# Row requests of a product-key expert layer in another order: the first table one group ahead, the second table with sixteen slots at the end

## What is computed

```python
def one_chunk(xc):                      # 128 tokens
    q = (xc @ w_query).reshape(C, 8, 2, 128)
    s = einsum('chpd,hpnd->chpn', q, subkeys)
    s1, i1 = top_k(s[:, :, 0], 16); s2, i2 = top_k(s[:, :, 1], 16)
    top_s, top_c = top_k(all sums of s1 and s2, 16)
    idx = i1[top_c // 16] * 128 + i2[top_c % 16]
    act = gelu(einsum('chkd,cd->chk', u_tbl[idx], xc))
    coef = softmax(top_s) * act
    return einsum('chk,chkd->cd', coef, v_tbl[idx])
```

## Time and profile before

| | |
|---|---|
| time, median of 3 runs | 1553.29 us (1553.16 to 1553.7) |
| time of the profiled execution | 1554.89 us |
| its span on the core | 1553.1 us |

### The profile page before, as it was taken

One profiled execution on the slowest core, in us unless ns is written; L12 is line 12 of the kernel. 1 busy time (PEld: TensorE's weight loads), 2 busy tenths in 40 slices (PEclk: granted clock), 3 DMA queues, 4 the chain that ended last, 5 costly groups with the idle time before them and its releaser, 6 DMA issues.

```text
span 1553.1 us, 13591 instructions
## 1 busy us (share of the span) xinstructions
PE 1035.4 (67%) x4216; PEld 471.9 (30%) x4216; DVE 1036.3 (67%) x2716; ACT 397.5 (26%) x920; POOL 974.2 (63%) x1041
## 2 busy tenths in 40 slices
PE   9998877655846767736675688787757774444444
PEld 8984422221213332212221334333212221111111
DVE  3367667775777484837676757377778677767673
ACT  1122132222222323222321232333222332112122
POOL 0067757776766655756666665467757767777772
PEclk9999978887967987878887788988979787766667
DMA  9699999999999999999999999999999999999996
GB/s 330 200 343 391 406 406 409 407 406 403 409 409 406 398 405 402 382 407 405 407 406 404 385 401 402 396 373 409 406 406 409 409 410 409 410 409 409 409 409 243
DMA packets 194636, 607.57 MB, mean 391 GB/s; under 512 B 17596, under 2 KB 44292, under 8 KB 194564
## 3 DMA queue, kind: packets, MB, share of 16 engines
q0 software_dynamic: 147456, 536.94, 87.3%
q1 hardware_dynamic: 46976, 69.73, 12.7%
q10 hardware_dynamic: 132, 0.04, 0.0%
HBM read 605.59 MB, written 1.05 MB: 391 GB/s over the span
## 4 chain that ended last, share of the span: by engine, by line
DMA 35%; PE 21%; POOL 17%; DVE 14%; issue 8%; ACT 5%; DVEq 0%; POOLq 0%; ACTq 0%
DMA rows<-in_peer_u,expert 18%; DMA rows<-in_peer_v,expert_v 16%; POOL rows L682 10%; PE sums L967 8%; DVE rows L1820 7%; POOL rows L675 7%; PE banks L783 4%; PE banks L799 4%; DVE coef L1837 2%; ACT soft_diag L1346 1%; PE banks L792 1%; PE sums L792 1%; DMA wring<-in_attn_w_q 1%; PE banks L775 0%; ACT L1331 0%
## 5 line engine op out<-in xcount | busy, mean ns | idle before, releaser
L967 PE MATMUL sums<-rows,soft_diag 128*64 128x512 f32 x2048 | 583.6, 724 | 446.9 <-ACT soft_diag L1346 446.6
L1820 DVE SCALAR_TENSOR_TENSOR rows<-rows,xn_near 128x1024 f32<-128x1024 f32 x512 | 612.6, 1219 | 253.3 <-DMA rows<-in_peer_u,expert 241.3
L682 POOL DMA_INDIRECT rows<-in_peer_v,expert_v x512 | 489.6, 956 | 295.4 <-PE sums L967 159.0
L675 POOL DMA_INDIRECT rows<-in_peer_u,expert x512 | 481.9, 941 | 258.9 <-issue 126.5
L967 PEld LDWEIGHTS sums<-rows,soft_diag 128*64 128x64 f32 x2048 | 162.7, 164 | 841.9 <-ACT soft_diag L1346 541.1
L1346 ACT ACTIVATE soft_diag<-stacked,coef 128x64 f32<-128x64 f32 x512 | 160.7, 343 | 369.8 <-DMA rows<-in_peer_v,expert_v 296.7
L1338 ACT ACTIVATE gelu<-dots 128x8 f32<-128x8 f32 x64 | 13.3, 208 | 446.1 <-DVE rows L1820 444.2
L799 PE MATMUL banks<-wring,xT 128*128 128x512 f32 x160 | 77.3, 636 | 3.4 <-DMA wring<-in_attn_w_q 3.4
L1837 DVE SCALAR_TENSOR_TENSOR coef<-gelu,gate_inv,gate 64x4 f32<-64x4 f32 x256 | 56.8, 222 | 23.4 <-ACT gelu L1338 19.5
L1885 DVE SCALAR_TENSOR_TENSOR soft_diag<-banks,soft_diag 128x512 f32<-128x512 f32 (+1 forms) x8 | 7.7, 958 | 92.7 <-ACT soft_diag L1367 92.7
L783 PE MATMUL banks<-xT,rows 128*128 128x128 f32 x448 | 51.1, 276 | 1.3 <-issue 0.6
(11 more groups left out here) (230 smaller groups left out, 958.6 us busy)
## 6 DMA issues: line engine op xcount, KB each, us to landing
wring<-in_w_kv SPq DMA_DIRECT2D x14, 1024.0 KB, 16.9
rows<-in_peer_u,expert POOLq DMA_INDIRECT x512, 15.0
rows<-in_peer_v,expert_v POOLq DMA_INDIRECT x512, 14.4
wkept<-in_peer_w_query SPq DMA_DIRECT2D x8, 1024.0 KB, 13.7
rows<-in_conv_w_in SPq DMA_DIRECT2D x7, 1024.0 KB, 11.9
wring<-in_peer_w_query SPq DMA_DIRECT2D x7, 1024.0 KB, 13.1
wring<-in_attn_w_q SPq DMA_DIRECT2D x7, 1024.0 KB, 16.5
wkept<-in_conv_w_out SPq DMA_DIRECT2D x4, 1024.0 KB, 12.5
```

The costliest lines, as they stand in the source:

```text
L675: nc.gpsimd.indirect_dma_start(u_row[j], None, u_table, bass.IndirectOffsetOnAxis(ap=expert[n % 2][:, k:k + 1], axis=0)).then_inc(u_landed ...
L682: nc.gpsimd.indirect_dma_start(v_row[j], None, v_table, bass.IndirectOffsetOnAxis(ap=expert_v[n % 2][:, k:k + 1], axis=0)).then_inc(v_land ...
L967: last = nc.tensor.matmul(sums[side * HP:(side + 1) * HP, half, :], diag[:, g * GROUP + j, :], v_row[j][:, half * 512:(half + 1) * 512], s ...
L1820: nc.vector.scalar_tensor_tensor(out=u_row[j], in0=u_row[j], scalar=1.0, in1=xn_near[:, :, :].rearrange("p a d -> p (a d)"), op0=ALU.mult, ...
```

## The change

POOL's queue is put in another order. Before: u0 v0 u1 v1 u2 v2 u3 v3 ... (each a group of 8 rows). Now: u0 v0 u1, then row by row v(1, 0) u(2, 0) v(1, 1) u(2, 1) ..., then u3 v2 u4 v3 ... u62 v61, then row by row u(63, 0) v(62, 0) u(63, 1) ..., then v63. The wait for the experts of group 2 stands ahead of the first v(1, j). The number of gathers is the same, 512 of each table.

PE's `combine_in_slot(K)` takes group K for K = 0 and 1, nothing at K = 2, and group K-1 after that. ACT's `weigh(K)` now makes four diagonals of group K-1, the gelu of group K, and the other four (all eight first, at the last group). DVE makes the coefficients after the next experts have been found or after the slot's mixer work, where before it made them right after the dots. `expert_v`, the second table's indices, has three buffers where it had two.

From group 49 on, every second group of the second table goes into eight further slots, `spare_rows`, which lie in two thirds of the weight ring, `keyT` and `value`; a v pair then waits for `v_used` of the group before the last.

```diff
+        spare_rows = [a.rearrange("p a t -> p (a t)")[:, D * half:D * (half + 1)]
+                      for a in (wring[:, 0], wring[:, 1], keyT[:, :, :], value[:, :, :]) for half in range(2)]
...
+        FIRST_LATE = GROUPS
+        LAST_GROUP = GROUPS * STEPS - 1
...
-            first_group()
-            for K in range(1, GROUPS * STEPS):
-                gather_group(K // GROUPS, K % GROUPS)
+            def experts_of(K):
+
+                if K == 1:
+                    pool.wait_ge(expert_ready, 2)
+                elif K % GROUPS == 0:
+                    pool.wait_ge(expert_ready, K // GROUPS + (2 if K else 1))
...
+            def second_row(K, j):
+
+                n, g = divmod(K, GROUPS)
+                if j % 2 == 0:
+                    if K == TWO_SETS + 1:
+                        wait_filled(pool, "queries", 1, 1)
+                    elif K:
+                        pool.wait_ge(v_used, TWOS * (K - 1 if K <= TWO_SETS else K - 2) + j // 2 + 1)
...
+            first_rows(0)
+            second_rows(0)
+            first_rows(1)
+            experts_of(FIRST_LATE)
+            for j in range(GROUP):
+                second_row(FIRST_LATE - 1, j)
+                first_row(FIRST_LATE, j)
+            for K in range(FIRST_LATE + 1, LAST_GROUP):
+                first_rows(K)
+                second_rows(K - 1)
+            second_experts_of(LAST_GROUP - 1)
+            for j in range(GROUP):
+                first_row(LAST_GROUP, j)
+                second_row(LAST_GROUP - 1, j)
+            second_rows(LAST_GROUP)
...
+            def combine_in_slot(K):
+
+                if K != FIRST_LATE:
+                    n, g = divmod(K if K < FIRST_LATE else K - 1, GROUPS)
+                    combine(n, n % 2, g)
...
+                K = GROUPS * n + g
+                early = GROUP if K == LAST_GROUP else GROUP // 2
+                if K > FIRST_LATE:
+                    diagonals(K - 1, range(early))
                 act.wait_ge(dot_done, TOPK * n + ks.stop)
                 nc.scalar.activation(gelu[b][:, ks], dots[b][:, ks], ACT.Gelu).then_inc(gelu_done, 1)
+                if K > FIRST_LATE and early < GROUP:
+                    diagonals(K - 1, range(early, GROUP))
+                if K < FIRST_LATE:
+                    diagonals(K, range(GROUP))
```

More of the change, by code:

```diff
@@ L439, in trunk @@
         expert = [sb(f"expert{b}", [P, TOPK], U32) for b in range(2)]
-        expert_v = [sb(f"expert_v{b}", [P, TOPK], U32) for b in range(2)]
+        expert_v = [sb(f"expert_v{b}", [P, TOPK], U32) for b in range(3)]
         top = [sb(f"top{b}", [P, TOPK]) for b in range(2)]
@@ L527, in trunk @@
         u_landed = [sem(f"u_landed{j}") for j in range(U_SLOTS)]
-        v_landed = [sem(f"v_landed{j}") for j in range(V_SLOTS)]
+        v_landed = [sem(f"v_landed{j}") for j in range(2 * V_SLOTS)]
         bank_done = sem("bank_done")
@@ L682, in gather_v @@
                 nc.gpsimd.indirect_dma_start(
[L683 to L701, removed]
@@ L703, in gather_group @@
-            def gather_group(n, g):
-                K = GROUPS * n + g
+                    v_at(GROUPS * n + g, j), None, v_table,
+                    bass.IndirectOffsetOnAxis(ap=expert_v[n % 3][:, k:k + 1], axis=0)).then_inc(v_landed[v_slot(GROUPS * n + g, j)], 16)
+            def experts_of(K):
                 if K == 1:
                     pool.wait_ge(expert_ready, 2)
-                elif g == 0:
-                    pool.wait_ge(expert_ready, n + 2)
-                for j in range(GROUP):
[L711 to L718, removed]
@@ new lines, in first_rows, with second_rows @@
+            def first_rows(K):
+                experts_of(K)
+                for j in range(GROUP):
+                    first_row(K, j)
+            def second_rows(K):
+                second_experts_of(K)
+                for j in range(GROUP) if K else (6, 7, 0, 1, 2, 3, 4, 5):
+                    second_row(K, j)
+            first_rows(0)
[5 more added lines that the diff above has]
+                first_row(FIRST_LATE, j)
@@ L1245, in _ @@
             query_pair(1, 3)
-            combine(2 * first + 1, 1, 0)
+            combine_in_slot(first + 2)
             turn_pair(1, 3)
             score_pair(1, 3)
[L1249 to L1252, removed]
+            for K in range(first + 3, GROUPS * STEPS + 1):
+                combine_in_slot(K)
             assert taken[0] == len(fills) and halved[0] == len(halves)
@@ L1622, in _ @@
             weigh_pair(STEPS // 2 - 1, last=True)
+            diagonals(GROUPS * STEPS - 1, range(GROUP))
             nc.scalar.preload_act_table_set("natural_log_exp_and_others")
@@ L1862, in step @@
                     find_experts(n + 1, at, 1 - b, layer)
+                if opens:
+                    add_chunk(n - 1, 1 - chunk)
             def second_group(n, b, chunk, norm=None):
@@ L1993, in _ @@
             second_group(0, 0, 0)
+            coefficients(0, 0, 1)
             conv_group(1, LATER[3])
@@ L1998, in _ @@
                     add_mixer(1)
+                coefficients(n, n % 2, 0)
                 second_group(n, n % 2, 0, ("ffn0", 1) if n == 2 else None)
+                coefficients(n, n % 2, 1)
             for c in range(CH):
@@ L2015, in _ @@
                     mixer_slot(c, t)
+                    coefficients(n, b, t % GROUPS)
             first = (STEPS - HEADS) // 2
@@ L2020, in _ @@
             norm_stream("final", 0)
+            coefficients(2 * first, 0, 0)
             second_group(2 * first, 0, 1)
+            coefficients(2 * first, 0, 1)
             step(2 * first + 1, 1, 1, HEADS + 2, 1, scored=("scoring", 1, 1))
+            coefficients(2 * first + 1, 1, 0)
             second_group(2 * first + 1, 1, 1)
+            coefficients(2 * first + 1, 1, 1)
             for i in range(first + 1, STEPS // 2 - 1):
```

64 lines of the change are left out of this document (42 added, 22 removed).

## The result

| | before | after |
|---|---|---|
| time, median of 5 runs | 1553.70 us (1553.16 to 1553.94) | 1564.74 us (1564.38 to 1565.05) |
| time of the profiled execution | 1554.89 us | 1564.73 us |
| its span on the core | 1553.1 us | 1563.0 us |

The ratio is 1.0070, with a 95% interval of 1.0058 to 1.0081. The spans differ by 9.9 us and the medians by 11.0, because the profiled execution of before was 1.2 us above its median and that of after was not.

A forecast was written before the change was run, and what follows sets the result against it. One DMA engine behind the others was taken as the bound, so only early waits cost. 1553.1 us of span plus 6.8 and 2 gave 1561.9, or 1562.1 as median; the 8-in-10 range was 1553 to 1569.

The forecast's parts named there:

- The first hole: Queue empty near 121 us because v(1, 0) is issued later: +6.8 us, paid in full and never worked off.
- rival B: No change, 1554 us: the slow engine did idle at 955 and 1011 us, cancelling the early loss; chance 0.07.
- The bound: Rows land at the pace of one lagging DMA engine; from about 130 us its backlog makes the removed waits free.
- The wait ahead of v(1, 0): POOL waits for DVE's third expert count, issuing v(1, 0) at about 121.8 us: +6.8 us, low bound 5.8.
- The second hole: Before u(4, 0): interleaving makes v(1, 7) and then slot 1's scores late; 7 us less weight traffic, +2, bounds 0 and 7.
- Lead, later coefficients, buffers, sixteen slots: From group 4 on, and the slots from group 49: 0 us; bounds -2 and +4 for all but the slots.
- the 159 us mostly go: POOL's second-table waits for PE, 159.0 us before, would mostly vanish; the trace sign was well under half.
- The slices at 405 and more: Trace sign: the profile's middle slices would show 405 GB/s and more, and still no gain in time.
- The tail: After the last row lands, work on PE and DVE changes by 0 us, bounds -0.3 and +1.2.
- Rival A: The mean of the DMA engines is the bound, so the fuller queue gains up to 18.5 us: 1543.6, chance 0.15.
- D: Slower, 1571 us: gap before u(4, 0) in full (+7), and later mixer work stops POOL beyond its backlog (+4); chance 0.08.
- The sign given for the end: Trace sign: the same lone engine working at the end, and the last row landing at about 1553 us.

The follow-up runs named there:

- e5_stop_short: The kernel before, with four memsets of dead `keyT` stopping POOL ahead of u(56, 0) at 1363 us: 1553.89 us, ratio 0.9997 to before.
- e6_stop_long: The kernel before, with eight memsets of dead `keyT` stopping POOL ahead of u(56, 0): 1559.49 us, ratio 1.0035 to before.
- e2_wait_not_mixed: The changed kernel with the wait for group 2's experts kept, but v(1) and u(2) as whole groups: 1559.45 us, ratio 1.0038 to before.
- e3_wait_alone: The kernel before with only POOL's wait for group 2's experts added ahead of v(1, 0): 1560.04 us, ratio 1.0036 to before.
- e1_plain_start: The changed kernel with v(1) then u(2) as whole groups and no early wait for experts: 1553.78 us, ratio 0.9996 to before.
- e4_one_set: The changed kernel without the eight further slots `spare_rows`: 1564.78 us, ratio 1.0066 to before.
- e7_scores_first: The changed kernel with slot 1's queries and scores ahead of group 1's `combine` on PE and its diagonals on ACT: 1559.21 us, ratio 1.0032 to before.
- e8_stop_lead: The kernel of e1_plain_start with eight clearings of `wring[:, 2]` stopping POOL ahead of u(56, 0): 1557.42 us, ratio 1.0019 to before.

## Why the prediction was right, and where its terms were off

1562.1 us was forecast, with 1553 to 1569 around it; 1564.74 came. Direction, mechanism and place held; one term of the sum was too small by more than half. Two things helped the number. The first hole was put 1.1 us too high and the second 3.3 too low, so 8.8 us of change were forecast where 11.0 came. And the range was wide enough to hold rival B's no change too: that the mechanism is right rests on the runs, not on the range. (The 0.2 us between the span and the median says nothing: an execution takes 1.7 to 1.8 us more than its span, and the profiled one of before was long by 1.2 to 1.6.)

- **The bound** (one engine behind the others; waits shorter than its backlog are free): right, by e5_stop_short and e6_stop_long. The floor was taken too high: 5.5 to 6.0 were landings with something still queued, and with nothing queued it is 4.2 to 4.3. That makes the 6.7 us at 1011 us 2.5 above the floor, not 1.2, which speaks for the forecast.
- **The wait ahead of v(1, 0), +6.8**: it costs 5.7 in the medians of e2_wait_not_mixed and e3_wait_alone, and 6.0 in the landings. The issue came 6.72 later, as worked out. The term left out that the queue still had something to do when v(1, 0) was issued in before: that row landed 5.6 us after its issue, and lands after 4.2 now. So 1.4 of the 6.7 was covered, and the slower restart took part of that back. The low bound of 5.8 was right by size and for a reason of that kind.
- **The second hole, +2**: this is the step that was mis-sized; it cost 5.3, inside its bounds of 0 and 7. The chain on the engines was forecast well: scores read at 166.1 (166.2), experts at 174.8 (174.5), u(4, 0) landed at 183.05 (183), though that last agreement is luck: it was issued at 178.80 (177.3) and took 4.3 us (5.5). The queue wasn't. It ran dry at 173.36, not 174.5, and behind the hole the next two landings came after 2.28 and 2.16 us in place of 1.28, 1.9 us more. That is a gross hole of 10.3 where 7 stood; the weights filled their 5.1 as forecast, and the whole error fell on the small difference (5.2 by the landings). The restart after a dry queue, which is also the 1.5 us in e6_stop_long, was missing from the working altogether.
- **Lead, later coefficients, buffers, sixteen slots, 0**: right, by e1_plain_start (all of them) and e4_one_set (the slots). But "the 159 us mostly go" is wrong, and so is the sign "well under half": 103.6 are left, and the first table's waits for DVE doubled. Both were forecast from PE's side alone. POOL goes on only as slots come free, and what it no longer waits for at one table it waits for at the other.
- **The slices at 405 and more**: not met either. The dip that was 373 is now 355 and 387. One stop there is still 9 us and its first landing comes at 5.8:

```profile
1012.70 0.93 POOL L699 DMA_INDIRECT rows<-in_peer_v,expert_v  x1 [8.99 <-PE sums L1008]
```

- **The tail, 0**: right. From the last three diagonals to DVE's first addition it is 3.6 us, 3.8 before, and PE is at full clock in the window at 1552 us.
- **Rival A** (1543.6) fell twice over: its gain in bytes never came (e1_plain_start), and where bytes were lost the time stayed (e5_stop_short). Which of the sixteen engines is behind, and whether it is the same one throughout, the traces don't say. **B** fell with the landings of e3_wait_alone. Of **D** (1571) only one part came, the greater part of the second hole. The sign given for the end, last landing at about 1553 and the same lone engine, was met at 1554.0.

**The 1 to 2 us between rows 96 and 160** that the other kernels gain on before (5.6 to 4.2 in e3_wait_alone, 12.3 to about 10.3 in after) are not the work of the lead or of the wait. e5_stop_short and e6_stop_long are the kernel before up to 1363 us, and they gain 1.9 and 1.0 there too. In the profiled execution of before, rows 107 and 146 land 2.2 us after the row ahead in place of 1.28; after, e1_plain_start, e5_stop_short and e7_scores_first have neither of the two late landings, e3_wait_alone and e6_stop_long have one. So executions of one program differ by such steps, and the one of before has two more there than the one of after. It fits with the spans differing by 1.1 us less than the medians.

What stays open is what makes the steps. They are how the last engine falls behind: in before, between 1030 us and the end, its lag grows from about 2 to 9.5 us, mostly in eight steps of 0.94 to 1.01 (rows 650, 693, 747, 791, 843, 886, 942, 1003), and between the steps, where no weights are under way, the first engine's parts and the last one's both come every 1.28 us. Each of the eight landings, and those of rows 107 and 146, come 1.5 to 2.4 us after the start of an 8 KB packet on the instruction queue (q14 of the page, at 1046.2 and 1102.2 us for the first two). Six other such packets in that stretch have no step. That is a coincidence in time; no run tests it as a cause.

## What to carry to other kernels

Where rows land at the pace of one queue or engine, a wait ahead of it costs what it exceeds the backlog by, and the backlog can be read off directly: time from issue to landing, less the same with nothing queued. So sort the waits by that, not by their sum: here a stop of 8.7 us near the start, 6.7 of them new, cost 5.7, and one that added 7.4 at 1363 us nothing. When requests are interleaved, follow the one that becomes last to the engine that consumes it, and ask what stands behind that consumer in program order; and when a hole is costed as a difference, add the time that a dry queue takes to come back to pace.

## What the runs showed of the hardware

- The DMA engines don't move in step. The last one's part of a row lands up to 10.8 us after the first one's (row 609 of before), while at row 1022 the other fifteen are within 2.7 us; behind POOL's long stop at 1011 us the lag is 1.9, since the others stood still, and it then grows again to 9.5 at the last row, in steps of about 1 us and not by a slower pace. The Trainium skill ("DMA: Bandwidth & Descriptors", Latency and other measured facts) says that two of the 16 are usually slower, and gives contention for the gathers' descriptor rings as a guess. The lag is in these traces, of one engine in before and not of two; its cause is not.
- A 512 KB gather into a dry queue lands 4.2 to 4.3 us after its issue starts (121.70 and 178.80 us in after, 1366.66 in e8_stop_lead, 1377.52 in e6_stop_long). The Trainium skill's fit for such a transfer (the same page, Anatomy of one DMA), some 2.0 us and the bytes at 436 GB/s, would make it an estimated 3.2; the measurement is a microsecond over that.
- A queue that ran dry doesn't come back at full pace: 1.5 us (e6_stop_long), 1.8 (e8_stop_lead) and 1.9 (after, at 183 us) are lost over the one or two landings behind the first.
- POOL's clearing of 128 x 2048 floats took 1.86 us (14.86 / 8 in e6_stop_long).
